# Feature-major products: rounded weights meet both halves of the activations in one 512-column matmul, and VectorE sums the bank's halves

## The reference

```python
def cross_attention(h, mem_n, w_q, w_kv, w_o):
    q = (h @ w_q).reshape(bsz, seq, XA_HEADS, XA_HD)
    k, v = jnp.split(mem_n @ w_kv, 2, axis=-1)
...
def swiglu(h, w_gate_up, w_down):
    gate, up = jnp.split(h @ w_gate_up, 2, axis=-1)
    return (jax.nn.silu(gate) * up) @ w_down

def second_block(...):
    mem_n = rms_norm_2(mem, mem_norm_g)
...
        h = rms_norm_2(x, norm_g[l, 0])
        q, k, v, g, lr, u_f, u_h, u_s = jnp.split(h @ w_in[l], split_at, axis=-1)
...
        x = x + mix @ w_out[l]
        x = x + cross_attention(rms_norm_2(x, norm_g[l, 1]), mem_n, w_xq[l], w_xkv[l], w_xo[l])
        x = x + swiglu(rms_norm_2(x, norm_g[l, 2]), w_gate_up[l], w_down[l])
    return rms_norm_2(x, final_norm_g)
```

## Time and profile before

| | us |
|---|---|
| median of 3 runs | 3786.3 |
| lowest and highest | 3783.2, 3786.9 |
| span of the profiled execution, first to last instruction | 3776.6 |
| the profiled execution's own time | not listed beside the span |
| TensorE busy | 3522.4 |
| VectorE busy | 2039.3 |
| ScalarE busy | 1541.7 |

### The profile page before, as it was taken

How to read it: one execution, slowest core, us unless ns; L and a number is a source line. 1 busy time by engine, 2 the same in 40 slices (tenths; PEclk the granted TensorE clock), 3 DMA queues, 4 the chain that set the end, 5 groups by cost and what they waited for, 6 DMA issues and landing times. The chain is left out here.

```text
span 3776.6 us, 70993 instructions
## 1 busy us (share of the span) xinstructions
PE 3522.4 (93%) x31292; PEld 2922.0 (77%) x31292; DVE 2039.3 (54%) x3564; ACT 1541.7 (41%) x2599; POOL 247.0 (7%) x295
## 2 busy tenths in 40 slices
PE   6798999999999989899999899989999999999998
PEld 3576777777767767777887788658998899999887
DVE  1354465456444666764656465655444555555444
ACT  2343343344333433455543443435333444444433
POOL 0001111111011130011100000010000000000000
PEclk9999999999999999999999799899999999999999
DMA  9433343334323245433335444334553555555554
GB/s 378 157 115 102 105 121 108 95 118 124 102 85 103 71 152 192 156 123 101 101 114 178 156 150 134 106 106 158 188 169 132 167 180 181 182 182 180 190 185 161
DMA packets 349473, 548.57 MB, mean 145 GB/s; under 512 B 11724, under 2 KB 119916, under 8 KB 346988
## 3 DMA queue, kind: packets, MB, share of 16 engines
q1 hardware_dynamic: 346716, 538.78, 43.8%
q10 hardware_dynamic: 2448, 5.24, 0.4%
HBM read 535.86 MB, written 8.13 MB: 144 GB/s over the span
## 5 line engine op out<-in xcount | busy, mean ns | idle before, releaser
L301 PE MATMUL lane<-r,r 128*128 128x256 f32 (+1 forms) x8520 | 1506.4, 326 | 53.0 <-DVE r L259 43.0
L301 PE MATMUL bank<-r,r 128*128 128x512 f32 (+2 forms) x6360 | 1399.6, 359 | 61.5 <-DVE r L259 25.3
L301 PEld LDWEIGHTS lane<-r,r 128*128 128x128 f32 x8520 | 1279.2, 193 | 209.8 <-DVE r L259 48.0
L259 DVE TENSOR_TENSOR r<-ring,r 128x1024 fp32r<-128x1024 f32 x770 | 939.7, 1227 | 808.9 <-ACT r L298 807.5
L301 PEld LDWEIGHTS bank<-r,r 128*128 128x128 f32 x6360 | 1052.2, 195 | 262.7 <-ACT arena L298 30.6
L298 ACT ACTIVATE r<-ring 128x1024 fp32r<-128x1024 f32 x770 | 808.7, 1055 | 769.1 <-PE lane L301 572.3
L301 PE MATMUL lane<-arena 64*64 64x64 f32 (+4 forms) x12940 | 618.5, 252 | 44.6 <-issue 12.7
L301 PEld LDWEIGHTS lane<-arena 64*64 64x64 f32 (+3 forms) x12940 | 465.0, 138 | 208.4 <-issue 121.9
L298 ACT ACTIVATE arena<-lane 128x256 f32<-128x256 f32 (+3 forms) x578 | 249.1, 451 | 577.5 <-PE lane L301 453.5
L270 DVE COPY arena<-lane 128x256 f32<-128x256 f32 (+3 forms) x366 | 131.9, 361 | 281.4 <-PE lane L301 256.1
L259 DVE TENSOR_TENSOR arena<-arena 128x256 f32<-128x256 f32 (+7 forms) x568 | 260.1, 489 | 35.7 <-ACT arena L298 14.1
(11 more groups left out here) (94 smaller groups left out, 1233.6 us busy)
## 6 DMA issues: line engine op xcount, KB each, us to landing
ring<-in_w_gate_up SPq DMA_DIRECT2D x88, 1024.0 KB, 5.0
ring<-in_mod_w SPq DMA_DIRECT2D x73, 1024.0 KB, 5.2
ring<-in_ev_w_in SPq DMA_DIRECT2D x44, 1024.0 KB, 8.3
ring<-in_w_down SPq DMA_DIRECT2D x44, 1024.0 KB, 5.0
ring<-in_od_w_in SPq DMA_DIRECT2D x40, 1024.0 KB, 5.0
ring<-in_w_in SPq DMA_DIRECT2D x40, 1024.0 KB, 5.1
ring<-in_w_xkv SPq DMA_DIRECT2D x32, 1024.0 KB, 5.3
ring<-in_ev_w_out SPq DMA_DIRECT2D x28, 1024.0 KB, 5.2
```

Of the source, the lines that this page charges most:

```text
L259: return Nothing() if self.e is None else self.e.tensor_tensor(o, a, b, op)
L301: return Nothing() if self.e is None else self.e.matmul(o, l, r, start=start, stop=stop)
```

## The change

The halves of hF and mT become one array: Halves keeps for each k an access pattern over both, .both[k], of 2 x 256 columns (lo, then hi; both lie where they lay). In times_w, for the feats groups of M.fused, the rounded weights are the stationary operand of one matmul of 512 columns over .both[k], which fills the whole bank; the weights' lo half then meets the activations' hi half in 256 columns, added to the bank's first half. So a product has two matmuls, of 512 and 256 columns, for three of 256. A bank's value is now the sum of its halves, and VectorE makes it (folded: a tensor_reduce over two elements) for every tile of these groups; ScalarE's part in them is gone, but for the tanh, which reads SBUF. ff_gate is split in two steps: ff_gate_in for the four tiles first, then ff_gate. ff_up folds into one of two new buffers (M.utmp) ahead of its multiply. The diff, cut:

```diff
+class Halves:
+    def __init__(self, name, both, k, R):
...
+        r = R(both).rearrange("p (s k t) -> p s k t", s=2, k=k)
+        self.lo, self.hi = ([r[:, s, i, :] for i in range(k)] for s in range(2))
+        self.both = [r[:, :, i, :] for i in range(k)]
...
-    M.hF = Pair("hF", at(0, 4096), at(4096, 4096), KT, R)
+    M.hF = Halves("hF", at(0, 8192), KT, R)
...
+    M.fused = ("hF0", "hF16", "hF32", "mT")
...
         if u.k + u.m == g.kt:
+            if g.kind == "ff_gate":
+                for b, f in zip(g.banks, g.tiles):
+                    step("ff_gate_in", b, 4 * g.args[0] + f)
             for b, f in zip(g.banks, g.tiles):
                 step(g.kind, b, f, *g.args)
...
+                if g.feats and pair in M.fused:
+                    c = slice(f * P, f * P + P)
+                    pe.mm(M.bank[b[0]].rearrange("p (s t) -> p s t", s=2), hi[:, j, c], M.pairs[pair].both[kk], k == 0, False)
+                    i = pe.mm(M.bank[b[0]][:, 0:T], lo[:, j, c], M.pairs[pair].hi[kk], False, k == g.kt - 1)
                 else:
...
     def x_scores(h, qt, b):
         fresh(b)
+        pe.wait_ge(*at("xq", h, "dve"))
         for e in ("act", "dve"):
-            pe.wait_ge(*at("xq", h, e))
             pe.wait_ge(*at("kv", e))
...
+    def folded(b, dst, *names):
+        v.wait_ge(*at("halves", *b))
+        v.add_up(dst, M.bank[b[0]].rearrange("p (s t) -> p t s", s=2)).then_inc(*v.n(("free", *b), *names))
...
+    def qk_in(b, f):
+        folded(b, M.qk[:, f, :])
+        if f < 2:
+            own()
+            v.ts(M.qk[:, f, :], M.qk[:, f, :], 0.125, None, MUL).then_inc(*v.n())
...
-        v.wait_ge(*at("gla_ready", "act"))
+        v.wait_ge(*at("gla_ready", "dve"))
...
     def us_in(b, f, n):
-        if f % 2:
-            v.wait_ge(*at("rtm_read"))
-            copied(b, M.us[:, 4 * n + f, :])
+        v.wait_ge(*at("rtm_read"))
+        folded(b, M.us[:, 4 * n + f, :])
...
+    def uh_in(b, f, n):
...
+        folded(b, M.uhp[f][:, 1:257], ("uh", n, f))
...
+    def ff_gate_in(b, c):
...
+        folded(b, M.ff.x[:, c, :], ("ff_in", c))
     def ff_gate(b, f, n):
         c = 4 * n + f
...
         v.wait_ge(*at("ff_tanh", c))
-        v.stt(M.ff.x[:, c, :], M.ftmp[f % 2], 1.0, M.bank[b[0]][:, 0:T], ADD, MUL).then_inc(*v.n(("free", *b), ("ff_g", c)))
+        v.stt(M.ff.x[:, c, :], M.ftmp[f % 2], 1.0, M.ff.x[:, c, :], ADD, MUL).then_inc(*v.n(("ff_g", c)))
     def ff_up(b, f, n):
         c = 4 * n + f
-        full(b)
-        v.wait_ge(*at("ff_g", c))
-        v.stt(M.ff.x[:, c, :], M.ff.x[:, c, :], 0.5, M.bank[b[0]][:, 0:T], MUL, MUL).then_inc(*v.n(("free", *b), ("ff_u", c)))
+        if c >= 2:
+            v.wait_ge(*at("ff_u", c - 2))
+        folded(b, M.utmp[f % 2])
+        own()
+        v.stt(M.ff.x[:, c, :], M.ff.x[:, c, :], 0.5, M.utmp[f % 2], MUL, MUL).then_inc(*v.n(("ff_u", c)))
         split("ff", c)
...
-        a.act(M.ftmp[f % 2], M.bank[b[0]][:, 0:T], ACT.Tanh, scale=0.5).then_inc(*a.n(("ff_tanh", c)))
+        a.act(M.ftmp[f % 2], M.ff.x[:, c, :], ACT.Tanh, scale=0.5).then_inc(*a.n(("ff_tanh", c)))
```

More of the change, by code:

```diff
@@ L415, in __init__, with cols @@
         self.y, self.yc, self.ysq = q(2816), q(3072), q(3328)
+class Halves:
+    def __init__(self, name, both, k, R):
+        n = both.shape[1] // 2
+        t = n // k
+        self.name = name
+        self.x = both[:, 0:n].rearrange("p (k t) -> p k t", k=k)
+        self.raw = [self.x[:, i, :] for i in range(k)]
+        r = R(both).rearrange("p (s k t) -> p s k t", s=2, k=k)
+        self.lo, self.hi = ([r[:, s, i, :] for i in range(k)] for s in range(2))
+        self.both = [r[:, :, i, :] for i in range(k)]
+    def cols(self, k, tl=None):
+        c = slice(0, self.x.shape[2]) if tl is None else slice(tl * P, tl * P + P)
+        return self.hi[k][:, c], self.lo[k][:, c]
 class Pair:
@@ L674, in layout @@
     M.tm = [uhp_[:, 0:512], uhp_[:, 512:1024]]
-    M.mT = Pair("mT", at(M3, 4096), at(M3 + 4096, 4096), KT, R)
+    M.mT = Halves("mT", at(M3, 8192), KT, R)
     M.memr = at(M3 + 8192, 4096).rearrange("p (t n) -> p t n", t=2)
@@ L686, in layout @@
     M.ff = Pair("ff", at(MF, FT * T), at(M3, FT * T), FT, R)
-    M.ftmp = [at(MF + FT * T + T * i, T) for i in range(2)]
+    M.ftmp, M.utmp = ([at(MF + FT * T + T * i, T) for i in p] for p in ((0, 1), (2, 3)))
     M.fg = at(0, D)
+    M.fused = ("hF0", "hF16", "hF32", "mT")
     M.pairs = {"mix": M.mix, "h1l": M.h1l, "h1c": M.h1c, "gF": M.gF, "hF0": M.hF, "hF16": M.hF, "hF32": M.hF, "mF": M.mF,
@@ L1892, in times_w @@
                 pe.wait_ge(*at(pair, kk))
-                if g.feats:
+                if g.feats and pair in M.fused:
                     c = slice(f * P, f * P + P)
-                    r_hi, r_lo = M.pairs[pair].cols(kk)
-                    l_hi, l_lo = hi[:, j, c], lo[:, j, c]
-                    o = M.bank[b[0]][:, 0:T]
-                else:
[L1899 to L1904, removed]
+                    pe.mm(M.bank[b[0]].rearrange("p (s t) -> p s t", s=2), hi[:, j, c], M.pairs[pair].both[kk], k == 0, False)
+                    i = pe.mm(M.bank[b[0]][:, 0:T], lo[:, j, c], M.pairs[pair].hi[kk], False, k == g.kt - 1)
+                else:
+                    if g.feats:
+                        c = slice(f * P, f * P + P)
+                        r_hi, r_lo = M.pairs[pair].cols(kk)
+                        l_hi, l_lo = hi[:, j, c], lo[:, j, c]
+                        o = M.bank[b[0]][:, 0:T]
+                    else:
+                        l_hi, l_lo = M.pairs[pair].cols(kk, tl)
+                        r_hi, r_lo = hi[:, j, :], lo[:, j, :]
+                        o = M.bank[b[0]][:, 0:g.n]
+                    pe.mm(o, l_hi, r_hi, k == 0, False)
+                    pe.mm(o, l_hi, r_lo, False, False)
+                    i = pe.mm(o, l_lo, r_hi, False, k == g.kt - 1)
                 if j == u.m - 1 and (end or f == g.tiles[-1]):
-                    names = [("full", *b)] if end else []
+                    names = [("halves" if g.feats and pair in M.fused else "full", *b)] if end else []
                     i.then_inc(*pe.n(*names, *([("used", u.number)] if f == g.tiles[-1] else [])))
@@ L2817, in us_in @@
     def us_in(b, f, n):
-        if f % 2:
-            v.wait_ge(*at("rtm_read"))
-            copied(b, M.us[:, 4 * n + f, :])
+        v.wait_ge(*at("rtm_read"))
+        folded(b, M.us[:, 4 * n + f, :])
     def uf_in(b, f):
-        if f % 2:
-            v.wait_ge(*at("gla_zeros"))
-            copied(b, M.uf[:, f, :])
+        v.wait_ge(*at("gla_zeros"))
+        folded(b, M.uf[:, f, :])
+    def uh_in(b, f, n):
+        v.wait_ge(*at("uh_zeros"))
+        if n:
+            v.wait_ge(*at("uh_read", n - 1, f))
+        folded(b, M.uhp[f][:, 1:257], ("uh", n, f))
     def local_ready():
@@ L2984, in kf_in @@
     def kf_in(b, f, n):
-        if f % 2:
-            v.wait_ge(*at("mF_read"))
-            copied(b, M.kF[:, 4 * n + f, :])
+        v.wait_ge(*at("mF_read"))
+        folded(b, M.kF[:, 4 * n + f, :])
     def vr_in(b, tl, n):
@@ L2998, in xq_in @@
     def xq_in(b, f, n):
[L2999 to L3002, removed]
+        for e in ("dve", "act", "pe"):
+            v.wait_ge(*at("kv", e))
+        folded(b, M.qF[:, 4 * n + f, :])
     def xq_done(h):
@@ L3536, in fn_tokens @@
             .then_inc(*a.n(("r5_sq", "fo", tl)))
[L3538 to L3543, removed]
     def load_fg():
@@ L3618, in kv_done @@
         a.here("kv", "act")
[L3620 to L3627, removed]
     def x_scores(h, qt, b):
@@ L3649, in ff_gate @@
         c = 4 * n + f
-        full(b)
-        for e in ("dve", "act", "pe"):
-            a.wait_ge(*at("ff", e))
+        a.wait_ge(*at("ff_in", c))
         if c >= 2:
             a.wait_ge(*at("ff_g", c - 2))
-        a.act(M.ftmp[f % 2], M.bank[b[0]][:, 0:T], ACT.Tanh, scale=0.5).then_inc(*a.n(("ff_tanh", c)))
+        a.act(M.ftmp[f % 2], M.ff.x[:, c, :], ACT.Tanh, scale=0.5).then_inc(*a.n(("ff_tanh", c)))
     def ff_up(b, f, n):
@@ L3671, in scalar_program @@
         k_rows, v_rows, q_rows, hn_square, hn_scale, k_turned, q_turned, scores, p_turned, gate_heads, attended, norm1, rms,
-        rms_turned, lr_in, lr_turned, qk_in, vg_in, gla_ready, gl_gate, gl_spread, gl_scores, gl_norm, to_mix, us_in, uf_in,
-        fn_channels, fn_tokens, uh_in, load_fg, add_x, hy_one, hy_two, hy_taps, hy_sides, hy_filter, hy_rows, hy_there, hy_norm,
-        mem_done, kf_in, vr_in, kv_done, xq_in, xq_done, x_scores, x_turned, x_values, ff_go, ff_gate, ff_up, finish, fence, mark)}
+        rms_turned, lr_in, lr_turned, vg_in, gla_ready, gl_gate, gl_spread, gl_scores, gl_norm, to_mix,
+        fn_channels, fn_tokens, load_fg, add_x, hy_one, hy_two, hy_taps, hy_sides, hy_filter, hy_rows, hy_there, hy_norm,
+        mem_done, vr_in, kv_done, x_scores, x_turned, x_values, ff_go, ff_gate, ff_up, finish, fence, mark)}
     take["split"] = split_step
```

20 lines of the change are left out of this document (3 added, 17 removed).

## The result

The changed kernel takes 3851.0 us (median of four runs, 3843.9 to 3854.3) against 3784.8 before: a ratio of 1.0174, 95% interval 1.0159 to 1.0189, 66 us slower. The two profiled executions lie 73 us apart (spans of 3776.6 and 3849.7). I had forecast 3822, also slower, with a range to 3848.

The account below looks back on a forecast made before the run. TensorE, busy for 93% of the span, was taken as the bound. Products -32.4, up groups +35.5, gate groups +1.2, clock +12 and other groups +20 made +36 on 3786.3: 3822 us, range 3796 to 3848.

Parts of the forecast that it names:

- Up groups: Feed-forward up groups: folds lengthen the serial chain ahead of the next weights, +3.2 us in each of 11, 35.5 us.
- Gate groups: Feed-forward gate groups: next weights end at 5.6 us with 5.55 at hand, losing 0.1 each, 1.2 us over 11.
- The clock: Behind feed-forward up-group waits: granted clock falls to 1.2 GHz for 3.4 us in 7 of 10, costing 12 us.
- The products' gain: All 2432 changed products: two matmuls for three take 346.7 ns instead of 360, gaining 32.4 us.
- The waits of the other groups: Fused groups outside feed-forward: TensorE waits for VectorE's folds at group borders and ahead of scores, together 20 us.
- The borders of kf and xq: Three kf borders wait for the third tile's bank, 4.0 us; scores after four xq groups wait for all tiles, 6.0 us.
- No cover left: Feed-forward up groups: whatever is added to the serial chain ahead of the next weights is added to the time.
- ScalarE's relief: Bank emptying outside feed-forward: taking copies off ScalarE is worth nothing, as it is not what ends these waits.
- (a): Rival: the clock holds through the feed-forward waits, 12 us less, 3810 us; chance 0.15.
- (b): Rival: the fold on VectorE is cheap, 0.42 us as if priced by its results, 3793 us; chance 0.10.
- (c): Rival: the 13.3 ns belong to weight loads and vanish from both matmuls, product 320 ns, 3758 us; chance 0.08.
- (d): Rival: a moving operand in two pieces streams no faster than two matmuls, nothing gained, 3854 us; chance 0.07.

Follow-up runs that it names:

- Products alone: Kernel before with only the two matmuls per product, banks emptied as before from their first half, hi x hi term left out: 3770.8 us, 0.9964.
- contiguous halves: Changed kernel with the halves of each k side by side, so the 512-column moving operand is one piece: 3849.1 us, 1.0173 against the kernel before.
- four and four: Feed-forward-only change, spread and rounded late, with four tiles' 512-column matmuls first, then their four of 256: 3760.7 us, 0.9939 against the kernel before.

## Why the prediction was wrong

The direction and the mechanism held, and so did the sum of the waits. Two terms of the sum failed, the clock's falls and the products' gain. The forecast was too small by 30 us. Step by step:

- **Up groups: right.** Forecast: TensorE goes on 9.4 after the next group's start and loses 3.2 more than before. Measured: 9.39; the distance between its matmuls there is 3.84 to 4.00 for 0.754 to 0.757 before, +31 us in ten groups and 3 more behind the eleventh, for 35.5 forecast. The fold was taken at 0.69 and has 0.684. That the place of the chain, ahead of the next weights, is the cause is shown by moving it (3851 to 3793).
- **Gate groups: right.** The view lists no wait behind them. The 0.1 forecast for each is there behind some: at 3110.50, in the third unit, a step between matmuls is 0.34 us for 0.23.
- **The clock: the step that failed, and the largest part of the miss.** "One for 7 of 10 ... 12 us" counted falls behind the eleven up groups alone, one of 3.4 us each. Measured: a fall behind nine of ten waits and behind the eleventh, and seven of these ten of twice that length, 20 us in the stage and 2 to 3 behind it. It also left out the other stages altogether, where 21 us more at 1.2 GHz cost some 10. Falls stand behind three of the four xq waits, for instance, which are idle times of 2.0 us; the prediction's own row of a fall behind 2.01 (rows 9) could have said so. Together some 32 us for 12.
- **The products' gain: mis-sized.** "13.3 ns x 2432 = 32.4 us gained": in the changed kernel a product takes 351.9 ns on average outside the falls, so 8 ns are gained, some 20 us by estimate. Products alone gave 11 to 14. The 13.3 were right for a stream without waits (346.7 in three kernels) and wrong for one with them.
- **The waits of the other groups: right in sum.** 20 us forecast, 22.7 more idle time measured. The borders of kf and xq came near the reckoning: TensorE's matmuls are 1.80 apart at 2660.21 (1.69 late, forecast 1.69) and 2.25 to 2.31 at the scores (forecast 2.28 and a step of 0.12). The uh border at 2383 was reckoned by the folds' own time (2.4) and not by what stands ahead of them in VectorE's order; it added 3.2. How the rest of the 22.7 is shared out among the borders isn't worked out here. That the net came out at 24 us for 6 forecast (20 less 14 of gain) is mostly the clock's and the pace's doing.
- **"No cover left" and ScalarE's relief: right.** ScalarE is less busy and nothing got faster by it.

**The rivals.** (a), the clock holds, fell with the falls. (b), a cheap fold, fell with its 0.684; its own sum has a slip too, since 0.45 a tile makes a loss of 2.75 an up group and 23 us, not 2.6 and 21.5. (c), a gain beyond 13.3 ns a matmul, was seen in no run. (d), a two-piece operand that streams no faster, fell with the 351.9 ns in the changed kernel, and contiguous halves show that the two pieces cost nothing.

The Trainium skill (TensorE: Matmul & The Clock Gate, section "Wait — 56ns, not 53.3ns?") puts the fixed cost of a warm matmul at about 2.5 ns. No run here shows that: the products take 360, 346.7 and 353.3 ns, where 768 columns at 2.4 GHz are 320, so a matmul has 13.3 ns or more on top.

The parts of the miss in the two traces, which lie 73 us apart where 36 were forecast, are estimates from the numbers above: some 20 us from the clock, some 13 from the products' pace, next to nothing from the waits, and 5 from the first block, which the change doesn't touch. By the medians the miss is 30, and those 5 us between two executions say how far one trace can be split.

## What to carry to other kernels

Work added to an in-order engine costs what stands behind it: here 0.7 us a tile, on an engine busy for half of the time, cost 3.1 us a group, since the next weights' split was queued behind four such tiles. Put the work that frees banks with time to spare behind the work that feeds the bound engine, and spread it; then the same change won 19 us in the feed-forward stage (507.0 to 488.2, both spread). In the other groups, which take five banks in turn and were not spread, it lost; whether spreading would help there wasn't tried. A wait of TensorE has to be priced with what comes after it, the fall of its clock and a stream that can restart at the slower pace. Here each 3.1 us of added wait brought 2 us more by the falls.

## What the runs showed of the hardware that I had not expected

- A stream of float32r matmuls, 512 and 256 columns in turn, has two paces at full clock: 346.7 and 353.3 ns for the pair, with the same instructions in the same order. It holds one of them over hundreds of matmuls and goes over, either way, at a wait or at a delay of 0.1 us between two matmuls; without one it stayed at 346.7 for 1408 products in three kernels. Why is open; the layout of the operand isn't the cause, and with four and four instead of in turn it was 350.8.
- Idle times of 2.0 us (matmuls 2.25 to 2.31 apart) were followed by a fall of the clock behind three of four xq groups (3.4 us at 1.2 GHz each), where the kernel before, with 0.6 (0.89 apart), has no fall.
- Fifteen matmuls with zeros in each of ten waits made the kernel 21 us faster.
- TENSOR_REDUCE over pairs 1 KB apart in PSUM, 512 elements to 256, takes 0.684 us, as one with a single result does (0.692).
